# One stationary of 16 columns for the gate products of the delta stage, instead of two of 8

## What is computed

```python
off = GDN_CONV_CH
a = p[..., off + GDN_WIDTH:off + GDN_WIDTH + GDN_HEADS].astype(jnp.float32)
b = p[..., off + GDN_WIDTH + GDN_HEADS:].astype(jnp.float32)
log_a = -jnp.exp(a_log) * jax.nn.softplus(a + dt_bias)
beta = jax.nn.sigmoid(b)
```

## Time and profile before

| what | value |
|---|---|
| median of 3 runs | 3023.97 us |
| lowest and highest | 3009.19 and 3032.94 us |
| the profiled execution, its own time | 3027.42 us |
| its span, first to last instruction | 3025.7 us |
| mean granted TensorE clock in it | 0.968 |
| TensorE busy (matmul) | 2878.1 us |
| VectorE, ScalarE, GpSimd busy | 1923.7, 1306.1, 458.6 us |

### The profile page before, as it was taken

One profiled execution on the slowest core, in us unless ns is written; L12 is line 12 of the kernel. 1 busy time (PEld: TensorE's weight loads), 2 busy tenths in 40 slices (PEclk: granted clock), 3 DMA queues, 4 the chain that ended last, 5 costly groups with the idle time before them and its releaser, 6 DMA issues. The chain is left out here.

```text
span 3025.7 us, 55195 instructions
## 1 busy us (share of the span) xinstructions
PE 2878.1 (95%) x22459; PEld 2779.4 (92%) x22459; DVE 1923.7 (64%) x2679; ACT 1306.1 (43%) x2060; POOL 458.6 (15%) x575
## 2 busy tenths in 40 slices
PE   8799999998999999999999999998999999999998
PEld 8679998787999999999999889887989999999998
DVE  6657995785576666676676667676566644444554
ACT  1344446534354444444443444455443333333443
POOL 1002897110011111111110011121011000000000
PEclk6799999899999999999999999999999999999999
DMA  9657665633658787677774666575557755554544
GB/s 370 232 184 233 214 216 186 202 119 126 209 201 273 266 280 262 237 261 251 243 256 138 160 207 205 176 240 160 171 197 273 239 175 186 180 180 168 181 168 140
DMA packets 284224, 632.56 MB, mean 209 GB/s; under 512 B 24770, under 2 KB 45702, under 8 KB 283782
## 3 DMA queue, kind: packets, MB, share of 16 engines
q1 hardware_dynamic: 232400, 484.75, 47.7%
q0 software_dynamic: 40192, 142.63, 13.9%
q10 hardware_dynamic: 11446, 2.54, 0.6%
HBM read 627.77 MB, written 2.10 MB: 208 GB/s over the span
## 5 line engine op out<-in xcount | busy, mean ns | idle before, releaser
L1004 PE MATMUL accumulators<-h_parts,weight_parts 128*128 128x256 f32 x4672 | 1185.0, 285 | 16.8 <-DVE weight_parts L910 16.8
L1006 PE MATMUL accumulators<-h_parts,weight_parts 128*128 128x256 f32 x4672 | 1181.9, 285 | 0.0
L910 DVE TENSOR_TENSOR weight_parts<-weights,weight_parts 128x1024 fp32r<-128x1024 f32 x584 | 707.2, 1221 | 444.6 <-ACT weight_parts L836 443.8
L1004 PEld LDWEIGHTS accumulators<-h_parts,weight_parts 128*128 128x128 f32 x4672 | 905.0, 194 | 22.4 <-DVE weight_parts L910 22.3
L1006 PEld LDWEIGHTS accumulators<-h_parts,weight_parts 128*128 128x128 f32 x4672 | 905.5, 194 | 0.0
L836 ACT ACTIVATE weight_parts<-weights 128x1024 fp32r<-128x1024 f32 x584 | 600.7, 1054 | 649.0 <-PE accumulators L1006 296.1
L997 PE MATMUL accumulators<-h_parts,weight_parts 128*128 128x256 f32 x4672 | 763.1, 286 | 23.5 <-ACT weight_parts L836 13.6
L997 PEld LDWEIGHTS accumulators<-h_parts,weight_parts 128*128 128x128 f32 x4672 | 652.0, 194 | 28.8 <-ACT weight_parts L836 13.1
L1316 PE MATMUL accumulators<-in_h_parts,in_weight_parts 128*128 128x256 f32 x1024 | 262.0, 288 | 16.9 <-DVE in_weight_parts L1636 16.7
L1636 DVE TENSOR_TENSOR in_weight_parts<-weights,in_weight_parts 128x512 fp32r<-128x512 f32 x256 | 188.9, 749 | 110.6 <-ACT in_weight_parts L1475 110.3
L1318 PE MATMUL accumulators<-in_h_parts,in_weight_parts 128*128 128x256 f32 x1024 | 258.5, 284 | 0.0
(11 more groups left out here) (369 smaller groups left out, 2926.2 us busy)
## 6 DMA issues: line engine op xcount, KB each, us to landing
weights<-in_w_ff SPq DMA_DIRECT2D x128, 1024.0 KB, 6.6
weights<-in_w_in SPq DMA_DIRECT2D x80, 1024.0 KB, 6.2
h_t<-in_ada_w POOLq DMA_DIRECT2D x96, 512.0 KB, 5.7
weights<-in_ffn_w_gate SPq DMA_DIRECT2D x44, 1024.0 KB, 5.1
weights<-in_ffn_w_up SPq DMA_DIRECT2D x44, 1024.0 KB, 5.2
weights<-in_ffn_w_down SPq DMA_DIRECT2D x44, 1024.0 KB, 5.0
weights<-in_w_out SPq DMA_DIRECT2D x32, 1024.0 KB, 5.1
wide<-in_ada_w POOLq DMA_DIRECT2D x128, 256.0 KB, 3.9
```

Of the source, the lines that this page charges most:

```text
L910: ins = nc.vector.tensor_tensor(w[:, held:held + take, 1, :], core.ring[:, q % RING, k:k + take, :], w[:, held:held + take, 0, :].bitcast( ...
L1004: nc.tensor.matmul(accs[nt], w[:, held, 0, cols[nt]], xk[:, 1, :], start=False, stop=False, skip_group_check=True)
L1006: ins = nc.tensor.matmul(accs[nt], w[:, held, 1, cols[nt]], xk[:, 0, :], start=False, stop=(last and nt % 2 == 1), skip_group_check=True)
```

## The change

TensorE multiplies all 16 columns at once: one matmul a slot with a stationary of 128x16, into partitions 0 to 15 of one bank, columns 0 to 255. [...] ScalarE makes two copies behind slot 49: of 8 rows to `core.gates` and of all 16 rows to `both_gates`, a stretch of the tile `attn_t` (`A`) that is free then. Behind its slot 52 TensorE multiplies `both_gates` with columns 8 to 15 of the identity, one fp32 matmul, into a newly claimed bank ("betas"). ScalarE's Sigmoid reads that bank, behind slot 56 instead of 51. The semaphore `beta_ready`, for which nothing waited, goes.

```diff
--- before.py
+++ after.py
@@ -1158,7 +1158,7 @@
     head_slot = value_slot + 7
     mean_slot = head_slot + 8
     steps = ("sig_ready", "f_ready", "lf_ready", "k_ready", "scanned", "diff_ready", "exp_ready", "prod_ready",
-             "sq_ready", "rs_ready", "silu_ready", "convolved", "conv_act", "qk_squared", "qk_rooted", "z_ready", "softplus", "beta_ready", "gates_in",
+             "sq_ready", "rs_ready", "silu_ready", "convolved", "conv_act", "qk_squared", "qk_rooted", "z_ready", "softplus", "gates_in",
              "last_shift")
 
     qk_fill_slots = [head_slot + n for n in (-3, -2, -1, 1, 3, 5, 7, 9)]
@@ -1182,6 +1182,7 @@
                            "p (c z n) -> p c z n", c=1, z=2))
         ada = Ada(ctx, nc, core, [(w_ada, 0, 2 * NT, 1)], LAST, IN_1_ASLOTS, ring)
         gate_work = A[0:HH, 0:2, :, :].rearrange("p h c t -> p (h c t)")
+        both_gates = A[0:2 * HH, 2:4, :, :].rearrange("p h c t -> p (h c t)")[:, 0:SEQ]
         b = hT[:, HH:2 * HH, :].rearrange("p a b -> p (a b)")
         block = ctx.enter_context(nc.Block())
 
@@ -1211,12 +1212,14 @@
                 bank = for_heads.claim(pe, "gates", "act")
                 for n in range(KT):
                     yield from pace.until(GATE_SLOT + n)
-                    for z in (2 * n, 2 * n + 1):
-                        m, k = z // KT, z % KT
-                        ins = nc.tensor.matmul(ps[0:HH, bank, m * SEQ:(m + 1) * SEQ],
-                                               core.w_gates[:, k, m * HH:(m + 1) * HH], hT[:, k, :],
-                                               start=(k == 0), stop=(k == KT - 1), skip_group_check=True)
+                    ins = nc.tensor.matmul(ps[0:2 * HH, bank, 0:SEQ], core.w_gates[:, n, :], hT[:, n, :],
+                                           start=(n == 0), stop=(n == KT - 1), skip_group_check=True)
                 ins.then_inc(for_heads.filled, 1)
+                yield from pace.until(GATE_SLOT + KT + 8)
+                pe.wait_ge(for_heads.emptied["act"], for_heads.release_of("gates"))
+                bank = for_heads.claim(pe, "betas", "act")
+                nc.tensor.matmul(ps[0:HH, bank, 0:SEQ], core.ident[0:2 * HH, HH:2 * HH], both_gates, start=True,
+                                 stop=True, skip_group_check=True).then_inc(for_heads.filled, 1)
 
             def diagonal():
                 for n in range(4):
@@ -1374,8 +1377,13 @@
             def gates():
                 yield from pace.until(GATE_SLOT + KT + 5)
                 bank = for_heads.wait_filled(act, "gates")
-                nc.scalar.activation(core.gates[:], ps[0:HH, bank, :], ACT.Copy
+                nc.scalar.activation(core.gates[:, 0:SEQ], ps[0:HH, bank, 0:SEQ], ACT.Copy)
+                nc.scalar.activation(both_gates, ps[0:2 * HH, bank, 0:SEQ], ACT.Copy
                                      ).then_inc(for_heads.releases("act", "gates"), 1)
+                yield from pace.until(GATE_SLOT + KT + 12)
+                bank = for_heads.wait_filled(act, "betas")
+                nc.scalar.activation(core.gates[:, SEQ:2 * SEQ], ps[0:HH, bank, 0:SEQ], ACT.Sigmoid
+                                     ).then_inc(for_heads.releases("act", "betas"), 1)
 
             def forget():
                 yield from pace.until(38)
@@ -1386,10 +1394,6 @@
                 nc.scalar.activation(X[:, 1, :], X[:, 0, :], ACT.Ln).then_inc(s["lf_ready"], 1)
 
             def forget_gates():
-                yield from pace.until(GATE_SLOT + KT + 7)
-                act.wait_ge(for_heads.emptied["act"], 1)
-                nc.scalar.activation(core.gates[:, SEQ:2 * SEQ], core.gates[:, SEQ:2 * SEQ], ACT.Sigmoid
-                                     ).then_inc(s["beta_ready"], 1)
                 yield from pace.until(GATE_SLOT + KT + 14)
                 act.wait_ge(s["z_ready"], 1)
                 core.act.link(act, nc.scalar.activation(gate_work[:, SEQ:2 * SEQ], gate_work[:, SEQ:2 * SEQ], ACT.Exp))
```

## The result

The changed kernel takes 3004.64 us (median of 14 runs, 2996.45 to 3013.12) against 3020.46 us for the kernel before (14 runs, 3009.19 to 3032.94): ratio 0.9945 with a 95% interval of 0.993 to 0.996, so 15.8 us less, between about 12 and 21. The profiled execution has a span of 3004.1 us where before had 3025.7. The forecast was 6.4 us less. The profiled executions are single ones, and their spans differ by more than the medians do. The forecast had the sign, and it had what goes on in the gate stretch, but more than half of the gain comes from something that it left out.

The account below looks back on a forecast made before the run. The prediction took TensorE's own issue to bound the gate stretch. Gate products -6.94, turning product 0, transfers 0 and late Sigmoid +0.5 made -6.4 us, from a median of 3023.97 to 3017.6 us, range 3004 to 3031.

Parts of the forecast that it names:

- The gate products: TensorE's 16 gate slots: one matmul a slot instead of two saves 0.434 us each, 6.94 us in all.
- Rival (e): Gate slots: a 16-column stationary costs double, so nothing is gained; 3024.5 to 3025.2 us, chance 0.03.
- rival (c): Gate slots: each record costs its weight load as well, so 9.3 us less, 3014.7 us; chance 0.04.
- The turning product: TensorE's added matmul at slot 52: 0.70 us, covered by 0.86 us of idle time before slot 56, so 0.
- ScalarE's two copies: ScalarE behind the gates: two copies take 0.7 us, 0.13 more than the one now, and this is hidden.
- The late Sigmoid: ScalarE at slot 56: Sigmoid and table load, 1.70 us, delay slot 59, where TensorE loses about 0.5 us.
- rival (b): Slots 56 to 64: ScalarE's delays cost 2.8 us, leaving 4.1 us of gain, 3019.8 us; chance 0.10.
- Transfers among the gates: Weight ring in the gate stretch: refills have 8.6 us, the slowest landing near takes 7.4, so no cost.
- rival (a): Right behind the gates: weight DMA sets the pace and takes the gain, leaving 0 to 2 us, say 3023; chance 0.10.
- rival (d): Between 212 and 222 us: wider gaps drop TensorE's clock to 1.2 GHz, 5.1 us slower, 3029.1 us; chance 0.03.
- Behind the gates all is tied by semaphores to TensorE's and VectorE's own slots: Work behind the gate stretch: waits and refill issues trace back to engine slots, so all moves with the gates' end.
- Sum: Whole kernel: -6.94 + 0 + 0 + 0.5 = -6.4 us, 3017.6 us by the median, 0.2% less; chance 0.70.

Follow-up runs that it names:

- doubled: The changed kernel with every 16-column gate matmul issued twice, the second time into the unused half of the bank: 3022.98 us, 1.0009 of the kernel before.
- the first pair: The first single traced executions of the kernel before and of the changed kernel, laid side by side: spans of 3025.7 and 3004.1 us.
- pad_before_196: The kernel before with 196 more waiting instructions on TensorE's queue over slots 4 to 20, all products kept: 3010.44 us, 0.9954 of the kernel before.
- late_after_60: The changed kernel with 60 more waiting instructions on TensorE's queue from slot 207 on: 3014.20 us, 0.9981 of the kernel before.
- pad_after_60: The changed kernel with 60 more waiting instructions on TensorE's queue over slots 4 to 8: 3008.69 us, 0.9957 of the kernel before; timed again 3012.43, 0.9974.
- pad_after_128: The changed kernel with 128 more waiting instructions on TensorE's queue over slots 4 to 13: 3005.40 us, 0.9937 of the kernel before.

## Why the prediction was wrong in size, point by point

- **The gate products**, -6.94: right. 32 records 0.22 apart, a period of 2.16 us for a forecast of 2.15. From its slot 28 to its slot 44 TensorE takes 41.19 us in each of seven traces with the two products a slot and 34.46 in eleven with the merged one, -6.73; doubled has 41.30. Rival (e), a 16-column product at twice the cost, would have left 2.58, and rival (c), loads paid besides, 1.97. The Trainium skill ("TensorE: Matmul & The Clock Gate", Part 3: Packing small matmuls, What overlaps and what doesn't) has weight loads overlap running matmuls only where the row groups differ. The 0.217 of the prediction doesn't test that by itself, as it doesn't tell whether a load of 90 ns is a part of it. The split product does, and disagrees: its loads take 193 ns, use all 128 rows, and its matmuls start 0.12 us apart, so a load must overlap running matmuls:

```profile
L1319 PEld LDWEIGHTS accumulators<-in_h_parts,in_weight_parts 128*128 128x128 f32 x1024 | 197.5, 193 | 19.2 <-DVE in_weight_parts L1640 18.8
```

- **The turning product**, 0: right. It runs at 202.4, two records, and TensorE stands idle for 0.47 us ahead of slot 56 all the same. From slot 44 to slot 56 TensorE takes 18.7 us with it and 18.6 without, means over 12 and 8 traces.
- **ScalarE's two copies**, hidden: right; 0.62 us against a forecast of 0.7.
- **The late Sigmoid**, 0.5: the place right, the size too small. From slot 56 to slot 60 TensorE takes 216.55 - 207.97 = 8.58 us where it took 7.91, 0.67 more. From there to slot 64 it takes 6.65 in both, so the evictions are covered, as the prediction said, and rival (b) is out. The prediction followed VectorE's part of slot 59 alone; the loss is shared by slots 58 and 59. There is no drain ahead of the table load: 1.28 long, from 207.94, and the Sigmoid starts at 209.23. The Trainium skill ("ScalarE: Activation LUTs", What ACT_TABLE_LOAD costs) gives every switch a drain of about 1.38 us beside the load; this trace doesn't show it.
- **Transfers among the gates**, 0: right. No wait of ScalarE for weights there, and rival (a) is out. The clock stays at 1.00 from 156 to 224 us, so rival (d) is out too.
- **"Behind the gates all is tied by semaphores to TensorE's and VectorE's own slots ... All of it moves with the end of the gates."** This is the step that failed. The weights' issues are tied to slots, but the instruction fetches are not: they come by the count of TensorE's instructions. With 60 fewer, two fetches no longer meet the issue of a refill that ScalarE is about to need. In the phase this is worth 3.2 us by the means of the traces (3.95 in the first pair, at slot 208), in a kernel that removes no product (pad_before_196, 11.4 us less for the whole) as well as in those that do. The prediction priced the products removed by their time alone, and their count at nothing.
- **Sum.** -6.73 at the gates and +0.67 for the Sigmoid are -6.06 for a forecast of -6.4 (-5.97 in the first pair). With -3.2 by the fetches in the phase that makes about -9.3, against the measured -10.8 by medians and -8.6 by means at the end of the phase. The rest up to 15.8, some 5 to 7 us, arises behind it. late_after_60 shows that the fetches' place there matters and is large enough. Which transfer or which stage it is stays open: from slot 255 to the end the single traces lie between 2435 and 2451 us in no order that fits. Nor is it shown that the fetches are all of it: the changed kernel with its fetches put back (pad_after_60, timed twice) keeps 13.2 and 8.3 us, not 6.4.
- **The range**, 3004 to 3031, took its width from the scatter of single runs (23.7 us in three runs of before). The time, 3004.64, lies at its lower edge, beyond every case that was worked out.

## What to carry to other kernels

Removing or adding instructions on a full queue changes two things: the time that they take, and where every later instruction fetch falls. The second was of the size of the first here, and instructions that compute nothing bring it as well. Before a gain is put down to an edit, lay the kernel before with as many harmless instructions more or fewer beside it, and in the trace look for DMA issues that take longer than their kind, with a packet of the instruction queue beside them.

## What the runs showed of the hardware

- TensorE's instructions come in packets of 16 KB. 256 instructions more, as the pad builds them, add one packet (136 for 135 of before) and leave the later ones in place, so by these two numbers an instruction has 64 bytes. The profile page of the changed kernel counts the packets (queue, packets, MB, share):

```profile
q8 instruction: 134, 2.20, 0.3%
```

- A fetch that meets SP's issue of a 1 MB refill stretches the issue from 0.37 us to 0.85 to 1.51, and the landing is then 7.6 to 9.0 us. At the refill for slot 108 that is seen in eight traces, at that for slot 152 in six of them, and never there in the eight traces with fetches placed as in the changed kernel, where the landing takes 5.8 to 6.7 us and twice 7.8. Two weaker meetings (issues of 0.69 in doubled and 0.76 in pad_after_128) landed in 6.4 and 6.6. By what path 16 KB cost a transfer of 1 MB two microseconds, no run tells apart.
- Waits on semaphores long passed cost TensorE nothing that shows where they stand here, ahead of slots 4 to 25: with 256 instructions of them the kernel before takes 3018.46 us against 3021.86 (0.9977 to 1.0003).
- A 16-column fp32 product costs what an 8-column one costs against the same 256 columns: 32 of either take TensorE from slot 28 to slot 44 in 41.30 us (doubled) and 41.19 (before). Going over to the fp32 products and back costs 1.14 - 0.87 = 0.27 us a slot before and 0.72 - 0.43 = 0.29 after.
